# The four input projections of an RWKV-7 block in three f32r products each, one run per projection

## What is computed

```python
def rwkv7_time_mix(h, ...):
    xx = token_shift(h) - h
    lerp = lambda j: h + xx * mu[j]
    xr, xw, xk, xv, xa, xg = (lerp(j) for j in range(N_LERP))
    r = xr @ w_in[0]
    k = xk @ w_in[1]
    v = xv @ w_in[2]
    g = xg @ w_in[3]
...
    y = wkv7_scan(rh, heads(decay), kh, vh, kk, kk * ah)
    y = head_group_norm(y, lnx_w.astype(f32), lnx_b.astype(f32))
    bonus = (jnp.sum(rh * kh * r_k.astype(f32), axis=-1, keepdims=True) * vh)
    y = (y + bonus.reshape(bsz, t, D_INNER)) * jax.nn.silu(g.astype(f32))
    return y.astype(h.dtype) @ w_out, v_first
```

## Time and profile before

| | us |
|---|---|
| median of 3 runs | 4588.41 |
| lowest and highest | 4586.32 to 4594.85 |
| profiled execution | 4586.48 |
| its span in the profile | 4584.8 |
| mean granted clock of TensorE | 0.938 |

### The profile page before, as it was taken

One profiled execution on the slowest core, in us unless ns is written; L12 is line 12 of the kernel. 1 busy time (PEld: TensorE's weight loads), 2 busy tenths in 40 slices (PEclk: granted clock), 3 DMA queues, 4 the chain that ended last, 5 costly groups with the idle time before them and its releaser, 6 DMA issues. The chain is left out here.

```text
span 4584.8 us, 131580 instructions
## 1 busy us (share of the span) xinstructions
PE 4219.0 (92%) x58346; PEld 3217.2 (70%) x58346; DVE 2370.4 (52%) x5302; ACT 1315.9 (29%) x3044; POOL 274.1 (6%) x308
## 2 busy tenths in 40 slices
PE   7999999999999999998988999999969977877579
PEld 5888888888888888886777887888746643444344
DVE  4556555565555655554215543444255533688842
ACT  2233323332323223222213332232113312433221
POOL 1000000000000000000000000000000000111100
PEclk9999999999999999998999999999989988566789
DMA  2322222222222222221413333333211110000010
GB/s 74 92 68 79 63 88 68 83 64 78 77 79 68 79 68 77 70 79 50 127 37 110 96 96 83 101 96 96 55 42 28 23 37 9 1 1 0 0 46 37
DMA packets 520412, 289.54 MB, mean 63 GB/s; under 512 B 30256, under 2 KB 509728, under 8 KB 519904
## 3 DMA queue, kind: packets, MB, share of 16 engines
q1 hardware_dynamic: 519904, 281.88, 21.3%
HBM read 267.55 MB, written 12.58 MB: 61 GB/s over the span
## 5 line engine op out<-in xcount | busy, mean ns | idle before, releaser
L344 PE MATMUL a_bank<-a_lerps,a_wt 128*128 128x256 f32 x4096 | 1036.9, 393 | 2.4 <-DVE a_lerps L815 2.4
L344 PEld LDWEIGHTS a_bank<-a_lerps,a_wt 128*128 128x128 f32 x4096 | 731.0, 189 | 126.9 <-issue 21.2
L1208 PE MATMUL b_bank<-b_hR,b_wR 128*128 128x512 f32 x1024 | 399.8, 390 | 15.5 <-DVE b_wL L1213 15.5
L1208 PE MATMUL b_bank<-b_hL,b_wR 128*128 128x512 f32 x1024 | 399.7, 390 | 0.0
L1208 PE MATMUL b_bank<-b_hR,b_wL 128*128 128x512 f32 x1024 | 399.5, 390 | 0.0
L931 DVE TENSOR_TENSOR a_iv_X<-a_bank,a_iv_X 128x256 f32<-128x256 f32 x256 | 108.7, 425 | 413.3 <-PE a_bank L448 413.3
L1213 DVE TENSOR_TENSOR b_wL<-b_w,b_wR 128x1024 fp32r<-128x1024 f32 (+1 forms) x144 | 192.4, 1340 | 116.8 <-ACT b_wR L1296 104.0
L692 ACT ACTIVATE a_iv<-a_bank 128x512 f32<-128x512 f32 x192 | 114.7, 597 | 419.1 <-PE a_bank L454 266.2
L1208 PEld LDWEIGHTS b_bank<-b_hR,b_wR 128*128 128x128 f32 x1024 | 193.0, 188 | 56.0 <-issue 16.1
L1208 PEld LDWEIGHTS b_bank<-b_hL,b_wR 128*128 128x128 f32 x1024 | 192.9, 188 | 40.4
L1208 PEld LDWEIGHTS b_bank<-b_hR,b_wL 128*128 128x128 f32 x1024 | 193.0, 189 | 40.2
(11 more groups left out here) (441 smaller groups left out, 8156.7 us busy)
## 6 DMA issues: line engine op xcount, KB each, us to landing
a_wt<-in_a_w_in SPq DMA_DIRECT2D x256, 512.0 KB, 4.2
b_w<-in_b_w_in SPq DMA_DIRECT2D x128, 512.0 KB, 4.0
b_w<-in_b_w_out SPq DMA_DIRECT2D x16, 1024.0 KB, 5.6
rwkv_out<-a_ybuf SPq DMA_DIRECT2D x64, 128.0 KB, 5.7
m_w<-in_a_w_out SPq DMA_DIRECT2D x16, 512.0 KB, 4.0
s_wp<-in_w_in SPq DMA_DIRECT2D x12, 512.0 KB, 3.8
a_xtok<-in_x SPq DMA_DIRECT2D x4, 1024.0 KB, 7.1
m_two<-rwkv_out SPq DMA_DIRECT2D x16, 256.0 KB, 3.0
```

Source lines behind the costliest of these rows:

```text
L344: r = mm(o, wt[:, j, c, :], src[:, c, :], start=(c == 0), stop=(c == ND - 1))
L1208: m = nc.tensor.matmul(o, a, b, start=(first and i == 0), stop=(last and i == 2))
```

## The change

A projection is computed in three f32r products instead of one f32 product. Each interpolation x is split into its f32r rounding R (by ScalarE) and the rest L = x - R, also f32r (by GpSimd), and each weight likewise (R by ScalarE, L by VectorE). Then out = wR xR + wR xL + wL xR. There are single buffers of R and L for each projection, a ring of three tmp tiles of two chunks for the interpolations, and the weights keep a tile apiece. `xx` lies in the x tile. The interpolations go by pairs of chunks (a "unit"; k, r, g, v of four each), in steps 14 and 15 of a pass. Each projection is one unbroken run. The order of the chain's pieces, some banks and the semaphores change with it.

```diff
+        lerpR, lerpL = ({n: sb(f"lerp{x}_{n}", [P, ND, PASS], F32R) for n in "krgv"} for x in "RL")
+        wR, wL = ({n: sb(f"w{x}_{n}", [P, ND, P], F32R) for n in "krgv"} for x in "RL")
+        tmp = [sb(f"tmp{i}", [P, 2, PASS]) for i in range(3)]
+        wt = {n: sb(f"wt_{n}", [P, ND, P]) for n in "krgv"}
...
-                    if m % NF == 3 and m // NF + 1 < NPS:
+                    for i, name in enumerate(LERPS):
+                        if m:
+                            sp.wait_ge(s["wL"], (m - 1) * len(LERPS) + i + 1)
+                        sp.dma_start(wt[name][:, :, :], w_in[W_IN[name]][:, :, cols]).then_inc(s["w" + name], 16)
+                        if i == 0:
+                            if m:
...
+                def project(o, m, name, lo, hi):
+
+                    if lo == 0:
+                        pe.wait_ge(s["wL"], m * len(LERPS) + LERPS.index(name) + 1)
+                    if m % NF == 0:
+                        pe.wait_ge(s["lo"], unit(m // NF, name, (hi + 1) // 2 - 1) + 1)
                     for c in range(lo, hi):
-                        r = mm(o, wt[:, j, c, :], src[:, c, :], start=(c == 0), stop=(c == ND - 1))
+                        mm(o, wR[name][:, c, :], lerpR[name][:, c, :], start=(c == 0), stop=False)
+                        mm(o, wR[name][:, c, :], lerpL[name][:, c, :], start=False, stop=False)
+                        r = mm(o, wL[name][:, c, :], lerpR[name][:, c, :], start=False, stop=(c == ND - 1))
...
+                    prep, at = prepared(n)
+
                     chained = n * NCH + 1
                     pe.wait_ge(s["Sc"], chained)
+                    pe.wait_ge(s["S1E1"], ready)
+                    blocks(7, iv["E1"], iv["S1"])
+                    blocks(7, iv["S1"], iv["E1"], at=PASS).then_inc(s["pE2"], 1)
...
-                    if m is not None:
-                        low_rank(m)
-                        pe.wait_ge(s["vcp"], n + 1)
-                    fill(keys, 0, 2)
...
-                    fill(keys, 2, 6)
+                    turn(2, A)
+                    turn(2, bdt["B"], PASS).then_inc(s["trAB"], 1)
...
+                    if m is not None:
+                        low_rank(m)
                     if before is not None:
                         normed(n - 1)
-                    fill(keys, 6, ND)
-                    fill(receptance, 0, 2)
...
-                    fill(receptance, 2, 6)
+                    fill(keys)
...
-                    fill(receptance, 6, ND)
-                    fill(gate, 0, 2)
+                    fill(receptance)
...
-                    fill(gate, 6, ND)
-                    fill(vals, 0, 2)
+                    pe.wait_ge(s["trAB_out"], ready)
+                    fill(gate)
...
-                    fill(vals, 2, 5)
+                    fill(vals)
...
-                    fill(vals, 5, ND)
...
+                def round_weights(m, names=LERPS):
+                    for name in names:
+                        act.wait_ge(s["w" + name], 16 * (m + 1))
+                        sem, count = free(name, 0)
+                        act.wait_ge(s[sem], count + m)
+                        a(wR[name][:, :, :], wt[name][:, :, :], ACT.Copy).then_inc(s["wR"], 1)
+
+                def round_lerp(ps, name, i):
+                    n = unit(ps, name, i)
+                    act.wait_ge(s["tmp"], n + 1)
+                    sem, count = free(name, ps)
+                    act.wait_ge(s[sem], count)
+                    a(lerpR[name][:, 2 * i:2 * i + 2, :], tmp[n % 3][:, :, :], ACT.Copy).then_inc(s["hi"], 1)
...
+                    act.wait_ge(s["pE8"], ready)
+                    copy(iv["E2"], 7, "E8")
+                    lerps(15, ("r", 2), ("r", 3), ("g", 0))
+                    if m is not None:
                         decays(m, e)
-                    act.wait_ge(s["pE8"], ready)
-                    copy(iv["E2"], 2, "E8")
+                    lerps(15, ("g", 1), ("g", 2), ("g", 3))
                     if m is not None:
                         keys(m, e)
+                        if m + 1 < STEPS:
+                            round_weights(m + 1, "k")
...
                         bonus(m, e)
+                        if m + 1 < STEPS:
+                            round_weights(m + 1, "r")
+                    lerps(14, ("k", 0), ("k", 1), ("k", 2))
+                    lerps(15, ("v", 0), ("v", 1), ("v", 2))
+                    if m is not None:
                         gate(m, e)
+                    lerps(15, ("v", 3))
                     act.wait_ge(s["pP12"], ready)
                     copy_two(pr12, 4, "P12", scale=-1.0)
-                    prep, at = prepared(n)
+                    lerps(14, ("k", 3), ("r", 0), ("r", 1))
...
+                        if m + 1 < STEPS:
+                            round_weights(m + 1, "g")
                         vals(m, e)
+                        if m + 1 < STEPS:
+                            round_weights(m + 1, "v")
...
+                def low_lerp(ps, name, i):
+                    n = unit(ps, name, i)
+                    pool.wait_ge(s["hi"], n + 1)
+                    pair_of = slice(2 * i, 2 * i + 2)
+                    low(lerpL[name][:, pair_of, :], tmp[n % 3][:, :, :], lerpR[name][:, pair_of, :]).then_inc(s["lo"], 1)
...
+                    if prep and at == 14:
+                        for name, i in (("k", 0), ("k", 1), ("k", 2), ("k", 3), ("r", 0), ("r", 1)):
+                            low_lerp(prep, name, i)
+                    if prep and at == 15:
+                        for name, i in (("r", 2), ("r", 3), ("g", 0), ("g", 1), ("g", 2), ("g", 3)):
+                            low_lerp(prep, name, i)
+                        for i in range(ND // 2):
+                            low_lerp(prep, "v", i)
...
+                    for name, i in units:
+                        n = unit(ps, name, i)
+                        v.wait_ge(s["xx"], ps * ND + 2 * i + 2)
+                        if n >= 3:
+                            v.wait_ge(s["lo"], n - 2)
+                        for c in (2 * i, 2 * i + 1):
+                            mu = dcols[:, 1 + MU[name], c:c + 1]
+                            o = stt(tmp[n % 3][:, c % 2, :], xx[:, c, :], mu, hT[:, c, 1:PASS + 1], ALU.mult, ALU.add)
+                        o.then_inc(s["tmp"], 1)
+
+                def low_weights(m, names):
+                    for name in names:
+                        v.wait_ge(s["wR"], m * len(LERPS) + LERPS.index(name) + 1)
+                        tt(wL[name][:, :, :], wt[name][:, :, :], wR[name][:, :, :].bitcast(F32), ALU.subtract).then_inc(s["wL"], 1)
...
+                    if prep and at == 15:
+                        lerped(prep, ("g", 1), ("g", 2), ("g", 3))
                     add_to_x("X2", "pX2", "X1")
                     if m is not None:
                         rates(m, e2)
                     add_to_x("X4", "pX4", "X2")
                     if before is not None:
                         tail(n - 1, e2)
+                    if m is not None:
+                        low_weights(m, "gv")
                     add_to_x("X8", "pX8", "X4")
...
                         bonus_keys(m, e2)
+                    if prep and at == 14:
+                        lerped(prep, ("k", 0), ("k", 1), ("k", 2))
+                    if prep and at == 15:
+                        lerped(prep, ("v", 0), ("v", 1), ("v", 2))
...
+                        if m + 1 < STEPS:
+                            low_weights(m + 1, "kr")
+                    if prep and at == 14:
+                        lerped(prep, ("k", 3), ("r", 0), ("r", 1))
+                    if prep and at == 15:
+                        lerped(prep, ("v", 3))
...
+                    if prep and at == 14:
+                        lerped(prep, ("r", 2), ("r", 3), ("g", 0))
```

More of the change, by code:

```diff
@@ L170, in rwkv_block @@
         xtok = sb("xtok", [P, PASS // P, D])
-        xx = [sb(f"xx{i}", [P, PASS]) for i in range(2)]
+        xx = xtok[:, :, :].rearrange("p a b -> p (a b)").rearrange("p (c n) -> p c n", n=PASS)
         ybuf = [sb(f"ybuf{i}", [P, PASS]) for i in range(2)]
@@ L261, in steps, with unit, free @@
                 step(n, n % 2, n % NF, n + 1 if n + 1 < STEPS else None, n - 1 if n else None)
+        LERPS = "krgv"
+        MU = {"r": 0, "k": 2, "v": 3, "g": 5}
+        W_IN = {"r": 0, "k": 1, "v": 2, "g": 3}
+        UNITS = len(LERPS) * ND // 2
+        def unit(ps, name, i):
+            return ps * UNITS + LERPS.index(name) * (ND // 2) + i
+        def free(name, ps):
+            return {"k": ("pk", ps * NF), "r": ("prk", ps * NF + 1), "g": ("pg", ps * NF + 1), "v": ("pv", ps * NF + 1)}[name]
         def prepared(n):
@@ L389, in normed @@
                 def normed(n):
-                    there, copied, rates = n + 1, n + 2, min(n + 2, STEPS)
-                    pe.wait_ge(s["ta"], rates)
+                    there, copied = n + 1, n + 2
+                    pe.wait_ge(s["H"], there)
```

(51 more changed lines are left out.)

120 lines of the change are left out of this document (49 added, 71 removed).

## The result

| | kernel before | changed kernel |
|---|---|---|
| median, us | 4591.63 (4 runs) | 4687.33 (4 runs) |
| lowest and highest, us | 4586.32 to 4595.01 | 4676.79 to 4690.06 |
| span of the profiled execution, us | 4584.8 | 4674.6 |
| ratio, 95% interval | | 1.0205 (1.0185 to 1.0225) |

The changed kernel is 96 us slower; 82 us faster was forecast, and the range ended at 4590. The loss lies in the first stage: from the start of step 63 to the end it is 2451.1 us before and 2452.8 now. The page of the changed kernel: busy time, TensorE's slices, its granted clock, the queue that brings instructions. It answers to the earlier trace rows.

The account below looks back on a forecast made before the run. TensorE was taken to bound the kernel: 165 us gained in the steps, less 71 at the pass changes and 12.5 at the start, gave 82 us off 4586.5, so 4505 us, range 4435 to 4590.

Parts of the forecast that it names:

- 0.120 a record, 12.3 us for four runs: Projections in a step: 96 f32r records at 0.120 us plus 0.2 per run, 3.25 us less than the nine f32 pieces.
- A (0.111): Rival, projections and pass changes: f32r records cost 0.111 us and pass changes overlap better, about 4440 us; chance 0.16.
- C (0.227): Rival, projections: the stationary load binds at 0.227 us a record, a step takes 40.1 us, the kernel 5150; chance 0.05.
- Who is late: Handoffs in a regular step: nothing lost at X8, 0.16 us at X32, 0.33 at R, making 29.56 us.
- For pauses like the 0.5 us one I add 0.2: 29.76.: Regular step: 0.2 us added for pauses, 29.76 against 32.38 before, so 165 us gained over 63 steps.
- the signs of being wrong: VectorE's low parts ending after TensorE wants X8, issue pauses in most steps, or runs of over 3.6 us.
- Rival B: Step's piece without projections: TensorE runs dry of instructions, 1.07 us a step, 4560 us, or 4590 with further handoffs; chance 0.12.
- Rival D: Small matmuls without projections: TensorE's clock falls every step, 5 us at 1.2 GHz, 158 us more, 4663; chance 0.05.
- The pass changes: Steps 14 and 15, three times: waits of 18.8 us plus 5 for the clock each, 71 us lost together.
- S1 and E1: Step 15 of a pass: interpolation pairs at the head of VectorE's work delay these two chain results by 2.2 us.
- The start: Before step 0: rounding and GpSimd's 16 pairs at 1.3 us delay it to about 78, 12.5 us lost.
- rival E: Pass changes and handoffs cost twice the forecast price, 84 us more, 4585 us, no change; chance 0.06.

Follow-up runs that it names:

- spread: Changed kernel with its f32r parts kept, but TensorE's and ScalarE's step order and the banks of the kernel before: 4682.7 us, 1.0212 of the kernel before.
- oneprod: Changed kernel with two of the three products of each projection left out, 8 f32r records a run in place of 24: 4472.8 us, 0.9747 of the kernel before.
- ring5: Changed kernel with five buffers for unrounded interpolations in place of three, and the gate's last and the values' pairs reordered: 4647.1 us, 1.0138 of the kernel before.
- lowdve: spread2r with the interpolations' low parts made on VectorE in place of GpSimd, and the interpolations placed anew: 4560.7 us, 0.9942 of the kernel before.
- spread2r: spread with VectorE's low parts of gate and values behind X8 and X32, pieces regrouped, plus ring5's buffers and order: 4569.0 us, 0.9963 of the kernel before.

## Why the prediction was wrong

- **What bounds the kernel.** Right: TensorE did, and its busy time fell by 116.5 us over these steps (2066.8 to 1950.3).
- **0.120 a record, 12.3 us for four runs.** Right: 0.12, and 4 x 3.06 = 12.2. The rule of the Trainium skill that the prediction cites (a load is hidden only behind a matmul for other rows), with the estimate of 0.214 from it, fails in f32r at 256 columns too. Rivals A (0.111) and C (0.227) fall.
- **Who is late.** Right for a regular step: no wait for X8; R costs 0.17 (forecast 0.33). One regular step takes 29.7, as laid out; the next shortest takes 30.5. But the cover for VectorE's low parts was thin: spread and oneprod, which shorten the receptance run, lose it.
- **"For pauses like the 0.5 us one I add 0.2: 29.76."** This is the step that failed. With the turning of x a regular step should have been 29.9 on average; it took 32.49. In the 55 regular steps the pauses behind a fetch take 122.5 us, 2.2 a step where I gave 0.2, and the regular steps spend 48 us at the lower clock, for which I gave nothing and which costs at most half of that, 0.4 a step. Together that is 2.4 of the 2.6 missing; the 2.6 come to 148 us over the 57 steps outside the pass changes. Issue pauses in most steps are also one of the signs of being wrong that the prediction names.
- **Rival B** named this mechanism and its place, but priced it at 1.07 a step from one pause in the last step, took only the stretch ahead of the keys, and got a chance of 0.12. The blocks were in reach: the page of before has 427 of them, 16 KB each. 452 small matmuls in a row are three and a half blocks in some 12 us, with bursts of 96 in under a microsecond, and in the trace of before, too, no two blocks come less than 3.2 us apart, and the pauses of 0.5 and 1.07 us end 2.3 and 2.5 us after a fetch. The question was how fast the densest block passes, not whether one pause was seen.
- **Rival D** was right in sign only: the clock does fall, but for 119 us of the stage and not for 5 us a step.
- **The pass changes.** Forecast 90.2 us for steps 14 and 15 together, measured 94.7. X2 late by 7.20 (6.6), v3 by 6.38 (5.4), S1 and E1 by 2.08 (2.2). The 5 us for the clock in each may have been few: 72 us at the lower level in the three, which cost at most 36. What I had not seen is that GpSimd holds VectorE up.
- **The start.** Forecast step 0 at 78, measured 87.4. I let GpSimd make a low part each 1.30 us; a unit takes 2.1 us there, 16 of them from 44.72 to 78.35 (GpSimd's first and last low part, below), and the forecast let the last end at 69.8. More buffers gave nothing (ring5), one engine in place of two gave 4 us (lowdve).

```profile
44.72 1.27 POOL L798 TENSOR_TENSOR a_lerpL_k<-a_tmp,a_lerpR_k 128x512 fp32r<-128x512 f32 x1 [5.42 <-ACT a_lerpR_k L683]
...
76.83 1.52 POOL L798 TENSOR_TENSOR a_lerpL_v<-a_tmp,a_lerpR_v 128x512 fp32r<-128x512 f32 x1 [1.02 <-ACT a_lerpR_v L683]
```

The sum for the profiled execution: 57 x 2.6 = 148, pass changes 3 x 4.5 = 13.5, start 9.4, together 171, against a span that was 4674.6 where 4503 had been forecast.

Two slips in the prediction's figures change nothing: rival E comes to 4589 (4505 + 84) and not 4585, and VectorE was busy for 18.1 us a step before (1141.9 / 63) and not 17.6.

Left open: what decides when the granted clock falls (it fell in every kernel with pauses and, in these steps, never in the one without), whether 3.2 us is the least that the instruction queue can leave between fetches, and why fewer transfers brought fewer pauses. Of 31.2 us in the best kernels' steps, about 0.7 are still supply pauses; a finer mix of pieces was not tried.

## What to carry to other kernels

Large matmuls that stand between small ones do three things: their own work, cover for the handoffs, and time for the next instructions to arrive. Before they are shortened or gathered, count the instructions of the densest stretch that is left and compare its time with the spacing at which the instruction queue delivers. A cheaper piece of cover is a shorter one, so look again at what each engine does ahead of the result that ends the wait.

## What the runs showed of the hardware

- TensorE's instructions come in blocks of 256 (16 KB; 255.75 between fetches). Where TensorE stands for a block, it goes on 2.2 to 2.8 us after the fetch began (95 of 111 pauses); the transfer itself takes 1.07 us. No two fetches in eleven kernels began less than 3.2 us apart, which is 25 ns for each matmul with its load. 32x32 matmuls can start every 9 ns.
- An f32r record of 256 columns with a 128x128 load of its own costs 0.12 us in a run of 24; at the lower clock (the run at 599.1) they start every 0.21 us.
- VectorE's instructions with two operands in SBUF wait for GpSimd, those with one in PSUM don't. Timeline of VectorE and of GpSimd in spread2r; L928 reads a bank, L929 and L923 (0.42 us otherwise) don't:

```profile
580.31 0.41 DVE L928 TENSOR_TENSOR a_scr<-a_bank,a_scr 128x256 f32<-128x256 f32 x1
580.64 1.16 DVE L929 TENSOR_TENSOR a_scr<-a_scr 128x256 f32<-128x256 f32 x1
581.72 1.49 DVE L923 TENSOR_TENSOR a_scr<-a_scr 128x256 f32<-128x256 f32 x1
```

```profile
579.26 3.67 POOL L806 TENSOR_TENSOR a_lerpL_g<-a_tmp,a_lerpR_g 128x512 fp32r<-128x512 f32 x2
```

The Trainium skill ("SBUF — State Buffer", section "SBUF: two separate sides") says that VectorE with two SBUF inputs and GpSimd share one pair of ports, which the first to start holds for its whole instruction. The rows agree: L929 ends at 581.80 and L923 at 583.21, each 0.3 us after one of the two GpSimd instructions ended. A low part on GpSimd lengthens such an instruction by 0.75 to 1.1 us, more than the 0.68 us that VectorE takes for the low part itself.
